# Eight experts on one core: features turned on VectorE, column groups dealt by features, smaller fetches, and the common case placed first

## The reference

```python
def _swiglu(x, w1, w3, w2):
    return (jax.nn.silu(x @ w1) * (x @ w3)) @ w2

def _moe(x, w_router, w1, w3, w2):          # w1, w3: 8 x 1024 x 3584, w2: 8 x 3584 x 1024
    ...
    logits = (xt @ w_router).astype(jnp.float32)
    top_v, top_e = lax.top_k(logits, TOP_K)             # TOP_K = 2, N_EXPERTS = 8
    gates = jax.nn.softmax(top_v, axis=-1)
    ...                                                  # rows sorted by expert, blocks of 128 rows
    yb = lax.map(run, (buf.reshape(n_blocks, EXPERT_BLOCK, D), block_e)).reshape(P, D)
    y = jnp.zeros((T, D), x.dtype).at[stok].add(yb[dest] * sg[:, None].astype(x.dtype))
```

## Time and profile before

| | |
|---|---|
| median of 3 runs | 2682.72 us (2681.34 to 2685.76) |
| profiled execution, whole | 2682.92 us |
| profiled execution, span from first to last instruction | 2681.1 us |
| TensorE busy | 2587.8 us, 97% of the span |
| VectorE busy | 1241.0 us, 46% |
| ScalarE busy | 969.5 us, 36% |
| GpSimd busy | 181.7 us, 7% |
| moved by DMA | 639.98 MB, mean 239 GB/s |

### The profile page before, as it was taken

The page is one execution under the profiler, slowest core; times in us unless marked ns, Lnnn a source line. Parts: engine busy times, 40 slices in busy tenths (PEclk is TensorE's granted clock), DMA queues, the critical chain, the costliest instruction groups (busy, mean ns, idle before and its releaser), DMA issues.

```text
span 2681.1 us, 66962 instructions
## 1 busy us (share of the span) xinstructions
PE 2587.8 (97%) x30946; PEld 2040.6 (76%) x30946; DVE 1241.0 (46%) x1650; ACT 969.5 (36%) x1339; POOL 181.7 (7%) x185
## 2 busy tenths in 40 slices
PE   8999999999989999999999999999899999989999
PEld 7977899897776666666666666588779978877997
DVE  6677655657750000000000001377567867756685
ACT  4555433355530000000000000256446645654563
POOL 1001000000000000000000000101600000160000
PEclk9999999999999999999999999999999999999999
DMA  6345755454459999999999999752134445313443
GB/s 219 136 160 191 291 180 181 137 199 164 151 192 396 393 391 413 388 412 392 398 404 390 412 387 416 289 171 104 50 119 174 165 173 187 111 50 112 164 177 108
DMA packets 99851, 639.98 MB, mean 239 GB/s; under 512 B 11664, under 2 KB 17296, under 8 KB 29808
## 3 DMA queue, kind: packets, MB, share of 16 engines
q1 hardware_dynamic: 85392, 598.61, 58.5%
q0 software_dynamic: 8352, 34.28, 4.3%
q10 hardware_dynamic: 5824, 2.75, 0.3%
HBM read 630.75 MB, written 13.24 MB: 240 GB/s over the span
## 4 chain that ended last, share of the span: by engine, by line
PE 80%; DVE 11%; ACT 4%; issue 3%; DMA 1%; SPq 0%; DVEq 0%; ACTq 0%
PE ps L1008 32%; PE ps L734 13%; PE ps L736 13%; PE ps L735 13%; DVE wlo L1919 3%; ACT whi L1450 1%; DMA raw<-in_units_dram 1%; PE ps L1308 1%; PE ps L1132 1%; ACT s L1802 1%; PE ps L1287 1%; PE ps L1319 1%; DVE s L2278 0%; DVE mx L2240 0%; PE ps L942 0%
## 5 line engine op out<-in xcount | busy, mean ns | idle before, releaser
L1919 DVE TENSOR_TENSOR wlo<-raw,whi 128x2048 fp32r<-128x2048 f32 (+5 forms) x250 | 531.5, 2134 | 307.6 <-ACT whi L1450 307.0
L1008 PE MATMUL ps<-raw,xe 128*32 128x256 f32 x10752 | 593.2, 379 | 3.6 <-DVE xe L2031 2.6
L1008 PEld LDWEIGHTS ps<-raw,xe 128*32 128x32 f32 x10752 | 359.7, 110 | 221.9 <-issue 11.5
L1450 ACT ACTIVATE whi<-raw 128x2048 fp32r<-128x2048 f32 (+4 forms) x252 | 447.8, 1780 | 204.4 <-PE ps L736 188.1
L736 PE MATMUL ps<-xTh,wlo 128*128 128x256 f32 x1480 | 418.2, 283 | 0.0
L2461 DVE TENSOR_TENSOR hb<-ps,hb 128x384 f32<-128x384 f32 x56 | 31.2, 557 | 834.4 <-ACT hb L1628 834.4
L735 PE MATMUL ps<-xTl,whi 128*128 128x256 f32 x1480 | 417.4, 282 | 0.0
L734 PE MATMUL ps<-xTh,whi 128*128 128x256 f32 x1480 | 417.1, 282 | 0.0
L1008 PE MATMUL ps<-raw,hTe 128*32 128x256 f32 x5376 | 293.4, 379 | 0.0
L734 PEld LDWEIGHTS ps<-xTh,whi 128*128 128x128 f32 x1480 | 280.2, 189 | 0.8 <-issue 0.7
L735 PEld LDWEIGHTS ps<-xTl,whi 128*128 128x128 f32 x1480 | 278.5, 188 | 0.1
(11 more groups left out here) (585 smaller groups left out, 3293.8 us busy)
## 6 DMA issues: line engine op xcount, KB each, us to landing
raw<-in_units_dram SPq DMA_DIRECT2D x544, 1024.0 KB
raw<-in_units_dram SPq DMA_DIRECT2D x18, 512.0 KB
raw<-in_units_dram SPq DMA_DIRECT2D x6, 768.0 KB
raw<-in_units_dram SPq DMA_DIRECT2D x8, 544.0 KB
raw<-in_units_dram SPq DMA_DIRECT2D x6, 688.0 KB
g<-in_b_gate_dram POOLq DMA_DIRECT2D x16, 256.0 KB, 8.0
raw<-in_units_dram SPq DMA_DIRECT2D x4, 576.0 KB
rows_y<-yb ACTq DMA_DIRECT2D x14, 144.0 KB, 5.7
```

What stands on the lines that cost most here:

```text
L1008: ins = self.e.matmul(bands(ps[r:r + 32, 256 * i:256 * i + 256]), G.x[:, kk, o:o + 32], w[:, k, :, c:c + 128], start=(kk == 0 and i != 1), ...
L1450: self.e.activation(self.m.hi[u % NHL][:, 0:n], self.m.raw[u % NRAW][:, 0:n], ACT.Copy) \
L1919: self.e.tensor_tensor(self.m.lo[u % NHL][:, 0:n], self.m.raw[u % NRAW][:, 0:n], self.m.hi[u % NHL][:, 0:n].bitcast(F32), ALU.subtract) \
```

## The change

- `rounds`: for `e13`, in round i all four bands now take the same token group i and band b takes the weight columns 128 b to 128 b + 127. For `e2` the dealing stays as it was.
- With that, a 32x32 block of `hb` holds 32 tokens by 32 features on any group of 32 partitions. VectorE turns these blocks itself, 128 x 384 elements in one instruction behind its product, and writes `hTe` (semaphore `hTd`). TensorE's step `across` and ScalarE's copies are gone in the narrow version. The features come out in another order, so the rows of w2 are laid out in that order when the weights are prepared.
- `lift` turns 96 token rows in place of 128, and for experts 1 to 7 POOL fetches one piece of 96 rows in place of two of 128. POOL gets a branch of its own for it.
- For expert 0 VectorE copies its half of `xe` first and does the gate's third part (`gated(2)`, lines 2482 and 2484) after it.
- TensorE alone places the narrow version first, behind a test for at most 96.
- The expert's rows are stored by two DMAs with longer pieces instead of four; `combine` reads them in the new order, with two instructions in place of one.
- `awake` does eight multiplications instead of six at the start of the second block.

```diff
@@ class Tensor
+    def experts(self, j0, j1):
+        ...
+        with self.e.If(self.most <= SLOTS):
+            self.tiles = 1
+            for j in range(j0, j1):
+                self.step(j)
+        ...
+        with self.e.Else():
+            self.tiles = 2
+            ...
-        self.awake(ps, {("n0", 0): 6, ("f20", 1): 3, ("f21", 1): 3}.get((tag, t), 0))
+        self.awake(ps, {("n0", 0): 8, ("f20", 1): 3, ("f21", 1): 3}.get((tag, t), 0))
@@ rounds
                 r, c, o = 32 * b, 128 * (i if b < 3 else 3), 32 * (b if b < 3 else i)
+                if g[0] == "e13":
+                    c, o = 128 * b, 32 * i
@@ whole
-            e.wait_ge(*self.at("hTe", ex, j // 2))
+            e.wait_ge(*self.at("hTd" if self.tiles == 1 else "hTe", ex, j // 2))
@@ lift
+        n = SLOTS if self.tiles == 1 else 128
-                ins = e.transpose(ps[:, k * 128:k * 128 + 128], m.xg[:, 0, k * 128:k * 128 + 128], m.ident[:, :])
+                ins = e.transpose(ps[:, k * 128:k * 128 + n], m.xg[0:n, 0, k * 128:k * 128 + 128], m.ident[0:n, 0:n])
@@ across (TensorE)
-        ps = self.fill(("ac", ex, cb), ("hTe", ex, cb))
+        ps = self.fill(("ac", ex, cb), ("hTd" if self.tiles == 1 else "hTe", ex, cb))
+        if self.tiles == 1:
+            return
-            for k in range(3):
-                ins = e.transpose(ps[:, k * 128:k * 128 + 128], m.hb[:, cb % 2, 0, k * 128:k * 128 + 128], m.ident[:, :])
@@ across (ScalarE)
-                e.activation(m.hTe[:, 4 * cb:4 * cb + 3, 0:96], ps[:, :, 0:96], ACT.Copy)
-                ins = e.activation(m.hTe[:, 4 * cb + 3, 0:96].rearrange("p (i n) -> p i n", i=3), ps[:, :, 96:128], ACT.Copy)
@@ storing an expert's rows (ScalarE's queue)
-                    for c in range(2):
-                        e.dma_start(cols[0:96, 0:3, c], yy[0:96, :, c]).then_inc(*self.c.up("stored", by=16))
-                        e.dma_start(cols[0:96, 3, c].rearrange("(i p) n -> p i n", p=32), yy[96:128, :, c]) \
-                            .then_inc(*self.c.up("stored", ("stored", ex), by=16))
+                    e.dma_start(rows[0:96, 0:768], m.yb[0:96, 0, 0:768]).then_inc(*self.c.up("stored", by=16))
+                    e.dma_start(rows[0:96, 768:1024].rearrange("(i p) n -> p i n", p=32),
+                                m.yb[96:128, 0, 0:768].rearrange("p (i n) -> p i n", i=3)) \
+                        .then_inc(*self.c.up("stored", ("stored", ex), by=16))
@@ lift (VectorE)
+            e.wait_ge(*self.at("full", "xe", a[0], 1))
+            n = SLOTS if self.tiles == 1 else 128
+            e.tensor_copy(m.xe[:, 4:8, 0:n], bands(self.psum("xe", a[0]), 8)[:, 4:8, 0:n]) \
+                .then_inc(*self.up("d_moe", ("xe", a[0], 1)))
             if a[0] == 0:
                 self.gated(2)
@@ product of an expert (VectorE)
+                e.wait_ge(*self.prev)
+                e.transpose(m.hTe[:, 4 * cb:4 * cb + 4, 0:96].rearrange("p s (i n) -> p i s n", i=3),
+                            m.hb[:, cb % 2, 0, 0:384].rearrange("p (i s n) -> p i s n", i=3, s=4)) \
+                    .then_inc(*self.up("d_turn", ("hTd", ex, cb)))
@@ index (POOL)
+            if ex and self.tiles == 1:
+                self.taken("xg0", ("xg", ex, 0), m.xg[0:SLOTS, 0, :], w["xd"], m.idx[0:SLOTS, 0:1])
+                return
             for h in range(2):
                 self.taken(f"xg{h}", ("xg", ex, h), m.xg[:, h, :], w["xd"], m.idx[:, h:h + 1])
```

More of the change, by code:

```diff
@@ L2883, in run @@
         self.load(("cmask",), m.cmask[:, :], a["c_cmask"])
-        for step in self.p.order:
-            self.do(step)
+        super().run()
     def do(self, step):
@@ L2954, in do @@
             e.wait_ge(*self.at("full", "e13", 7, 0))
-            for h in range(2):
+            for h in range(self.tiles):
                 e.wait_ge(*self.at("xg", 7, h))
```

91 lines of the change are left out of this document (57 added, 34 removed).

## The result

The changed kernel takes 2647.79 us, the median of 4 runs between 2646.34 and 2648.38 us. Beside it the kernel before took 2683.82 us (4 runs). The ratio is 0.9861, with a 95% interval from 0.9848 to 0.9874: 36 us faster, 1.4% by the ratio. The forecast was 2647 us. That the number came out within a microsecond is luck: the terms for the turning and the lift were 5.9 us too large, and 4.7 us that nobody had booked came in far behind the experts. The rest of this text is about that.

| us | before | after | gained | forecast |
|---|---|---|---|---|
| up to the experts' first unit | 793.85 | 789.09 | 4.8 | 4.1 |
| the experts' stage | 919.8 | 894.4 | 25.4 | 31.9 |
| behind it | 967.5 | 962.1 | 5.4 | -0.2 |
| span | 2681.1 | 2645.5 | 35.6 | 35.8 |

The account below looks back on a forecast made before the run. TensorE's queue was taken to bound the kernel, busy 97% of the span. Gains of 33.0 + 0.8 + 2.3 + 1.7 less 1.8 and 0.2 made 35.8 us, from 2682.9 to 2647 us, range 2643 to 2653 us.

Parts of the forecast that it names:

- e13: TensorE's 224 matmul units of the experts' first matrices; a unit longer than one of `e2` would show the forecast wrong.
- e2: TensorE's matmul units of the experts' w2, the yardstick that a unit of `e13` was not to exceed.
- The turning: Experts' column blocks: 56 blocks lose three TensorE transpositions each, 0.59 us a block, 33.0 us; VectorE's added block transpositions cost nothing.
- Lift: Transpositions of the next expert's rows, 96 columns wide instead of 128: 0.8 us gained, bounds 0 and 1.8.
- The weights' stream: Weight loads in the experts: no stall in experts 0 to 6; in the eighth, 1.8 us given back.
- Entering: Start of TensorE's narrow version: 2.3 us from falling through without a jump, 1.7 us from VectorE copying `xe` before the gate.
- Leaving: End of the experts: a 2.5 us jump in front of `awake` and sixteen records, net 0.2 us lost.
- The rest: Two stores instead of four on ScalarE's queue and fewer additions in `combine`, on engines that wait: nothing gained.
- Stream-bound in every expert: Rival: weights' stream held to 401 GB/s in the experts, an expert takes 112.9 us, total 2667 us; chance 0.10.
- Only the transpositions' own time: Rival: the 0.11 us a block stay and the exit jump shows in full; gain 26.8 us, 2656 us; chance 0.11.
- A slower dealing: Rival: first-matrix units grow as all four bands stream different weight columns; at 10% growth 2705 us; chance 0.04.

Follow-up runs that it names:

- b_same: The kernel before, word for word, profiled a second time: 2680.4 us (one run).
- u_lift: The changed kernel with the lift over 128 token rows again instead of 96: 2647.5 us, ratio 0.9855 to the kernel before.
- u_join: The changed kernel with the index for the expert after next moved right behind the lift in experts 1 to 6: 2644.3 us, ratio 0.9853 to the kernel before.
- u_fetch: The changed kernel fetching 2 x 128 rows for each expert again instead of 96: 2644.8 us, ratio 0.9852 to the kernel before.
- u_late: The changed kernel with the loads of the next stage's gains asked for behind unit 8 of the last w2: 2645.8 us, ratio 0.9859 to the kernel before.
- u_first: The changed kernel with TensorE's wide version of the experts placed first again, the narrow one last: 2651.8 us, ratio 0.9877 to the kernel before.
- u_gated: The changed kernel with VectorE's two gate instructions ahead of the copy of `xe` again at expert 0: 2650.5 us, ratio 0.9872 to the kernel before.
- u_awake: The changed kernel with six identity products in `awake` instead of eight: 2647.4 us, ratio 0.9854 to the kernel before.
- u_best: The changed kernel with both the index moved behind the lift and the gains' loads later: 2644.2 us, ratio 0.9850 to the kernel before.
- x_exit: The changed kernel with TensorE waiting for its last product of the narrow version before the jump out of it: 2653.5 us (one run).
- t_only: The kernel before with only the turning on VectorE and the new dealing of weight columns: 2655.5 us, ratio 0.9881 to the kernel before.

## Why the prediction was right, and which steps of it were not

**The turning, 33.0 us.** The bound was right (TensorE's queue), the cover was right (VectorE waits 13.9 us before each product), and the price of 0.59 us was right for a block whose transpositions stand alone. The step that failed is the factor 56. It took the price of a block whose transpositions stand alone for all blocks, and never asked which wait ends last where other work stands beside them:

- Three transpositions alone: 0.48 + 0.11 = 0.59 us. Gone, all gained; 42 blocks.
- Three transpositions and the index: 0.48 + 0.34 + 0.11 = 0.93 us (b_same). The index alone: 0.54 us. Gained 0.39, since the index costs 0.20 us more alone than beside them; 7 blocks.
- Three transpositions and the lift: 1.36 us, from 984.89 us to w2's first unit at 986.25 us in the chain. The lift alone: 0.81 + 0.49 = 1.30 us. Gained 0.06, since in both TensorE waits for VectorE's product of block 6; 7 blocks.

An expert thus gains 5 x 0.59 + 0.39 + 0.06 = 3.4 us, and 114.33 - 110.96 = 3.4 us was measured. Over the stage it is 24.8 + 2.7 + 0.4 = 27.9 us in place of 33.0 + 0.7. u_lift and u_join show the wait from both sides: a wider lift costs nothing, and an index beside the lift costs nothing. So 3.7 of the 5.1 us missing from the 33.0 went into a wait for VectorE, to whose side the forecast had booked "nothing". It had looked at the new instruction, whose result is wanted late, and not at the product before it, which frees the buffer. The other 1.4 us are 7 x 0.20 at the index. The Trainium skill ("TensorEngine Tiling (Array Packing)", Key Properties) has a drain at a change of the tiling mode, and I used it for 0.11 us a block; that the index and the transpositions share 0.20 us would fit it, but no run separates the drain from the rest of that price.

**Lift, 0.8 us.** Nothing in seven experts, since the lift lies inside the same wait. The first one, which has no product ahead of it, gave 0.2 us (1.03 to 0.85 us).

**The weights' stream.** I booked no stall in experts 0 to 6 and named one as a sign of being wrong; the profile of after has three, 1.2 us together, that of u_fetch none at 413 GB/s. The stream is at its edge, and small waits come and go. For the eighth expert I gave back 1.8 us; it was 3.45 - 0.93 = 2.5 against the first profile and 1.0 against b_same, which waits 2.5 us there. The mechanism was right, as u_late shows. All in all: 27.9 - 1.2 - 2.5 = 24.2 us, to which the first profile's longer block behind the index adds 7 x 0.27 = 1.9. That is 26.1 where 25.4 were measured; of the rest, the units of 2.599 instead of 2.597 us make 336 x 0.002 = 0.7.

**Entering, 2.3 + 1.7 us.** Right: 2.54 us of idle time went, u_first brought 2.64 back, and the wait for `xe` fell by 1.8 us. u_gated gives the pair 1.2 us of it, and 1.7 us more where the clock falls. The row fetch for expert 0 took the place of nothing in after, but was close: in u_awake, u_best and u_gated TensorE waited 0.19, 0.34 and 0.43 us for it.

**Leaving, -0.2 us.** The step that failed is the jump standing "in front of `awake`". It is there, and costs even more than I said, 5.18 us. But the sequencer reaches it while products are queued, and those cover it, in after just to the end. On entering less was covered: there the same kind of packet landed 1.39 to 1.47 us before TensorE went on, in all five profiles that have that jump. The Trainium skill ("Runtime: NRT & Kernel Launch", Instruction fetch mechanics) says that a taken branch out of the fetched pages must fetch its target, and the packets agree. The Trainium skill's 108 ns for a compare-and-branch ("Advanced Engine Details and Errata", Control Flow Timing) is not what these jumps cost; 2.54 us showed on entering and 5.18 us in x_exit. So `L893` is not late, and the clock kept up gives 0.7 us, inside my bound of 1.0.

**The rest, 0 us.** Here 4.7 us came in that I had not booked, all of it in the recurrence far behind the experts. The same instructions of VectorE last 0.68 us or 1.76 us there. Before, where the product `gm` begins 0.39 us after one of POOL's:

```profile
1914.99 1.59 POOL L3062 TENSOR_TENSOR R<-A,mk 128x512 f32<-128x512 f32 x1
1915.38 1.76 DVE L2759 SCALAR_TENSOR_TENSOR gm<-gm,mk 128x512 f32<-128x512 f32 x1
...
1917.19 1.15 PE L1281 MATMUL ps<-mk,gm 64*64 64x64 f32 x32 [1.03 <-DVE gm L2759]
```

After, where it begins 0.27 us ahead of POOL's:

```profile
1883.32 0.68 DVE L2794 SCALAR_TENSOR_TENSOR gm<-gm,mk 128x512 f32<-128x512 f32 x1
...
1883.59 1.55 POOL L3112 TENSOR_TENSOR R<-A,mk 128x512 f32<-128x512 f32 x1 [1.34 <-PE ps L1310]
...
1884.64 1.15 PE L1304 MATMUL ps<-mk,gm 64*64 64x64 f32 x32
```

TensorE waits 1.03 us for it in the one case and not at all in the other. The long one ends at 1917.14 us, 0.56 us after POOL's (1914.99 + 1.59), much as if it had been held until then. That this interplay makes the difference is read from the rows and no run changed it alone; what sets the order is open. It is not plain chance: three profiles of the before family lie at 966.4 to 967.5 us, ten with VectorE's turning (without x_exit) at 960.6 to 964.4 us, t_only among them, whose code behind the experts is the old one. No run told apart what of the turning tips it.

**The rivals.** Stream-bound in every expert: refuted, u_fetch moves 413 GB/s without a wait. Only the transpositions' own time: refuted, 26 units stand without a gap. A slower dealing: a unit of `e13` takes 2.598 to 2.599 us against 2.597 before, nothing that could be told. Had I taken 27.9 us for the turning and the lift together, and left the rest, the forecast would have been 2653 us.

## What to carry to other kernels

Before multiplying the price of one place by their number, ask at each place which wait ends last. Work of TensorE that stands where it waits for a buffer anyway is free: the lift and three transpositions, the lift alone and the lift with the index all took 1.3 to 1.4 us, because VectorE's product freed the buffer only then, while the index alone costs 0.54 us elsewhere. Taking work away there wins nothing, and moving work there wins its whole price. A long taken branch is best placed where the engine still has products queued: 5.18 us were just hidden behind them in after, up to 1.7 us showed in other versions, and 2.5 us or more on entering. And where the DMA share is 1.00, a gain on TensorE can come back in part as waits for weights: two edits of 3 us each gave 3 us together, by one profile of each.

## What was not expected of the hardware

- A jump of TensorE's program over a long part: 5.18 us with nothing queued, 2.5 to 2.8 us visible on entering, 0 to 1.7 us visible on leaving. A 16 KB packet of the queue "instruction" lies in it, and the first product behind the jump on leaving starts 1.60 to 1.63 us after that packet has landed, in nine profiles.
- Three full-width transpositions between runs of 32-column matmuls: 0.59 us; four products of two columns each: 0.54 us; both together: 0.93 us.
- The clock at its lower level behind 2.50, 2.64 and 2.80 us of idle time on entering, and not behind 2.54 and 2.56 us at the same place.
- The 32x32 block transposition of 128 x 384 on VectorE: 579 ns, about that of the product of the same shape (558 ns).
- One VectorE instruction (128 x 512) at 0.68 us or 1.76 us, by whether it begins 0.27 us ahead of POOL's or 0.39 us after it.
- The same program with an expert period of 114.61 us in one profile and 114.33 us in another, all of it in the column block behind the index.
